# Two routed mixtures: a turn's outputs added to the token sums by an indirect adding DMA in device memory

## What is computed

```python
def moe_swiglu(xn, router, w_gu, w_down):
    top_v, top_i = lax.top_k((xn @ router).astype(jnp.float32), TOP_K)
    w = jax.nn.softmax(top_v, axis=-1)
    comb = jnp.sum(jax.nn.one_hot(top_i, N_EXPERTS, dtype=jnp.float32) * w[..., None], axis=-2)
    out = jnp.zeros_like(xn)
    for e in range(N_EXPERTS):
        out = out + comb[..., e:e + 1] * swiglu(xn, w_gu[e], w_down[e])
    return out
```

## Time and profile before

| | |
|---|---|
| median of 3 runs | 2461.88 us (2461.0 to 2463.66) |
| the profiled execution | 2463.73 us, its span 2461.9 us |
| busy, of the span | PE 92%, PEld 77%, DVE 69%, ACT 54%, POOL 2% |
| mean granted TensorE clock | 0.954 |
| moved by DMA | 605.51 MB, mean 246 GB/s |
| first mixture, turns | about 764 to 1750 us |
| second mixture, turns | about 2145 to 2437 us |

### The profile page before, as it was taken

One profiled execution on the slowest core, in us unless ns is written; L12 is line 12 of the kernel. 1 busy time (PEld: TensorE's weight loads), 2 busy tenths in 40 slices (PEclk: granted clock), 3 DMA queues, 4 the chain that ended last, 5 costly groups with the idle time before them and its releaser, 6 DMA issues.

```text
span 2461.9 us, 29816 instructions
## 1 busy us (share of the span) xinstructions
PE 2261.1 (92%) x11321; PEld 1885.2 (77%) x11321; DVE 1694.6 (69%) x1551; ACT 1335.1 (54%) x1167; POOL 54.8 (2%) x64
## 2 busy tenths in 40 slices
PE   6989999897888999999999999999699789599996
PEld 6748999775676888888888888888589668588884
DVE  4325545576346888888888888888746514588986
ACT  4024333515335777777777777777554213377774
POOL 2000000000000000000000000000000000000000
PEclk9999999999888999999999999999889899599998
DMA  8243455531335999999999999999533242399993
GB/s 273 103 145 132 134 197 173 186 120 52 111 145 194 372 352 375 354 372 352 373 348 375 354 372 354 372 354 364 195 127 112 86 154 84 131 349 355 358 351 129
DMA packets 271625, 605.51 MB, mean 246 GB/s; under 512 B 9232, under 2 KB 34016, under 8 KB 271552
## 3 DMA queue, kind: packets, MB, share of 16 engines
q1 hardware_dynamic: 264944, 582.01, 65.9%
q0 software_dynamic: 6608, 22.49, 2.6%
HBM read 601.31 MB, written 3.15 MB: 246 GB/s over the span
## 4 chain that ended last, share of the span: by engine, by line
PE 79%; DVE 5%; ACT 4%; issue 2%; ACTq 0%; POOL 0%; DVEq 0%
PE ps L678 21%; PE ps L680 21%; PE ps L679 21%; PE ps L621 3%; PE ps L616 2%; DVE w_low L1978 1%; PE ps L940 1%; PE ps L842 1%; ACT w_high L1436 1%; PE ps L869 1%; PE ps L665 1%; PE ps L925 1%; PE ps L697 1%; ACT L1436 1%; PE ps L717 1%
## 5 line engine op out<-in xcount | busy, mean ns | idle before, releaser
L1978 DVE TENSOR_TENSOR w_low<-ring,w_high 128x2048 fp32r<-128x2048 f32 x432 | 983.7, 2289 | 142.2 <-ACT w_high L1436 141.4
L1436 ACT ACTIVATE w_high<-ring 128x2048 fp32r<-128x2048 f32 x432 | 824.0, 1916 | 178.3 <-PE ps L680 178.2
L679 PE MATMUL ps<-w_high,parts 128*128 128x512 f32 (+2 forms) x2024 | 788.9, 390 | 0.0
L678 PE MATMUL ps<-w_high,parts 128*128 128x512 f32 x1816 | 722.5, 398 | 29.7 <-DVE w_low L1978 15.1
L680 PE MATMUL ps<-w_low,parts 128*128 128x512 f32 x1816 | 711.1, 392 | 0.0
L679 PEld LDWEIGHTS ps<-w_high,parts 128*128 128x128 f32 x2024 | 382.7, 189 | 74.1
L678 PEld LDWEIGHTS ps<-w_high,parts 128*128 128x128 f32 x1816 | 342.7, 189 | 109.2 <-issue 24.4
L680 PEld LDWEIGHTS ps<-w_low,parts 128*128 128x128 f32 x1816 | 342.3, 189 | 73.3
L1589 DVE TENSOR_TENSOR w_low<-ring,w_high 128x2048 fp32r<-128x2048 f32 (+2 forms) x93 | 207.3, 2244 | 136.9 <-ACT w_high L1232 136.4
L678 PE MATMUL ps<-XT_high,w_high 128*128 128x256 f32 x896 | 259.0, 289 | 10.1 <-DVE parts L1578 6.2
L1232 ACT ACTIVATE w_high<-ring 128x2048 fp32r<-128x2048 f32 (+2 forms) x93 | 173.2, 1873 | 162.5 <-PE ps L680 123.2
(11 more groups left out here) (368 smaller groups left out, 1887.5 us busy)
## 6 DMA issues: line engine op xcount, KB each, us to landing
ring<-in_od_moe_gu SPq DMA_DIRECT2D x224, 1024.0 KB, 6.9
ring<-in_od_moe_down SPq DMA_DIRECT2D x112, 1024.0 KB, 6.7
ring<-in_w SPq DMA_DIRECT2D x96, 1024.0 KB, 7.2
ring<-in_ev_ffn_gu SPq DMA_DIRECT2D x22, 1024.0 KB, 7.5
ring<-in_xa_wkv SPq DMA_DIRECT2D x8, 2048.0 KB, 7.9
ring<-in_od_pw_w SPq DMA_DIRECT2D x6, 2048.0 KB, 8.7
ring<-in_w_in SPq DMA_DIRECT2D x6, 2048.0 KB, 8.0
ring<-in_ev_ffn_down SPq DMA_DIRECT2D x11, 1024.0 KB, 5.1
```

The source lines that it names most:

```text
L678: mm(out_, xh, wh, start=start, stop=False)
L679: mm(out_, xl, wh, start=False, stop=False)
L1436: A(w_high[:, j % SPLITS, :], ring[:, j % NS, :], ACT.Copy).then_inc(moe_sem(k, "high"), 1)
L1978: V.tensor_tensor(w_low[:, j % SPLITS, :], ring[:, j % NS, :], w_high[:, j % SPLITS, :].bitcast(F32), SUB)\
```

## The change

Inside the loops, the sums are no longer kept in on-chip memory. Ahead of each loop POOL stores `dst` in device memory (`sums`, with 128 spare rows behind the 256 token rows). At half 3 ACT copies the outputs of the turn before to `expert_out`, now in one float32 piece, and POOL issues an indirect DMA that adds these 128 rows to the rows of `sums` that `add_at` names; places of a turn without a token get a spare row. `find_rows` has one more column (`FILLED`), from which `places` on DVE computes the next turn's places (`next_at`), and `move_places` moves them to `add_at` at half 15, after the adding DMA of this turn has landed. In turn 0 all rows go to spare rows. The scatter matmuls, `outputs_low`, the four adds and the transposes of picks leave the loops. Behind a loop POOL reads the sums back to `dst`, and the last turn's outputs are added as before: `pick_last` makes its one-hot matrix once more, PE transposes it, scatters, and DVE adds after a wait for the sums.

```diff
-SCATTER_AT = (6, 8, 10, 11)
 TURN_PICKS_AT = 12
+FILLED = 5
+UNFILLED = 1024.0
...
-        gates = sb("gates", [P, 120])
+        gates = sb("gates", [P, 128])
...
+        rows_at, add_at, next_at = (sb(n, [P, 1], I32) for n in ("rows_at", "add_at", "next_at"))
+        expert_in, expert_out = w_(4096, D), w_(5120, D)
+        sums = {k: nc.dram_tensor(f"sums{k}", (T + P, D), F32, kind="Internal").ap() for k in (1, 2)}
...
-            def expert_rows(k, source, ready, value):
+            def expert_rows(k, source, ready, value, dst):
                 pool.wait_ge(S(ready), value)
                 pool.dma_start(row_store[k].rearrange("(a p) d -> p a d", p=P), source[:, :, :]).then_inc(S("rows_stored"), 16)
-                pool.wait_ge(S("rows_stored"), 16 * k)
+                if k == 2:
+                    pool.wait_ge(S("xs_ready"), 10)
+                pool.dma_start(sums[k][0:T, :].rearrange("(a p) d -> p a d", p=P), dst[:, :, :]).then_inc(S("rows_stored"), 16)
+                pool.dma_start(sums[k][T:T + P, :], dst[:, 0, :]).then_inc(moe_sem(k, "rows_added"), 16)
+                pool.wait_ge(S("rows_stored"), 32 * k)
+                pool.wait_ge(moe_sem(k, "rows_added"), 16)
                 pool.wait_ge(moe_sem(k, "turns_ready"), 1)
                 turns = pool.value_load(count[0:1, k - 1:k], min_val=MOES[k]["groups"], max_val=2 * MOES[k]["groups"])
                 with pool.Fori(0, turns) as it:
 
+                    pool.wait_ge(moe_sem(k, "outputs_by_act"), it + 1)
+                    pool.sem_inc(S("rows_asked"), 1)
+                    pool.indirect_dma_start(sums[k], bass.IndirectOffsetOnAxis(add_at[:, 0:1], 0), expert_out[:, :], None,
+                                            compute_op=ALU.add).then_inc(moe_sem(k, "rows_added"), 16)
                     pool.wait_ge(moe_sem(k, "rows_wanted"), it + 1)
...
+                pool.wait_ge(moe_sem(k, "rows_added"), turns * 16 + 16)
+                pool.sem_inc(S("rows_asked"), 1)
+                pool.dma_start(dst[:, :, :], sums[k][0:T, :].rearrange("(a p) d -> p a d", p=P)).then_inc(S("rows_back"), 16)
...
                             if half == 0:
                                 if ch == C - 1:
-                                    pe.wait_ge(moe_sem(k, "added"), it * 4 + 4)
                                     turn_rows(it + 1)
+                                if ch == 0:
+                                    pe.wait_ge(moe_sem(k, "outputs_by_act"), it + 1)
                                 pe.wait_ge(moe_sem(k, "hidden_split"), it * C + (ch + 1))
...
-                        if j in SCATTER_AT:
-                            scatter(it, SCATTER_AT.index(j))
-                        if j == TURN_PICKS_AT:
-                            turn_picks()
                         if j == ROWS_AT:
                             find_rows(it + 1)
 
+                turn_picks()
                 for i in range(4):
-                    scatter(turns, i)
-                pe.wait_ge(moe_sem(k, "added"), turns * 4 + 4)
+                    scatter(i)
+                pe.wait_ge(S("added"), 4 * k)
...
-                def outputs_high(turn):
+                def outputs(turn):
 
                     act.wait_ge(moe_sem(k, "read"), turn * N + SPLITS)
-                    A(y_high.rearrange("p (a n) -> p a n", a=2), ps[:, 2:4, :], ACT.Copy).then_inc(moe_sem(k, "outputs_by_act"), 1)
+                    act.wait_ge(moe_sem(k, "rows_added"), turn * 16 + 16)
+                    A(expert_out.rearrange("p (a n) -> p a n", a=2), ps[:, 2:4, :], ACT.Copy).then_inc(moe_sem(k, "outputs_by_act"), 1)
...
+                def places():
+
+                    V.tensor_scalar(next_at[:, :], ps[:, 7, FILLED:FILLED + 1], UNFILLED, SPARE, ADD, ALU.min)
+
+                def move_places(turn):
+
+                    dve.wait_ge(moe_sem(k, "rows_added"), turn * 16 + 32)
+                    V.tensor_copy(add_at[:, :], next_at[:, :]).then_inc(moe_sem(k, "places_moved"), 1)
+
                 def rows_wanted(turn):
                     dve.wait_ge(moe_sem(k, "rows_found"), turn)
+                    dve.wait_ge(moe_sem(k, "places_moved"), turn)
+                    places()
...
-                V.memset(picksT[:, :, :].bitcast(F32), 0.0).then_inc(moe_sem(k, "picks_ready"), 1)
                 pick(0)
                 gathered_low(0)
+                places()
...
                     for j in range(N):
-                        if j == EMPTY_AT:
-                            outputs_low(it)
-                        if j - 3 in SCATTER_AT:
-                            add(it, SCATTER_AT.index(j - 3))
                         if j == TURN_PICKS_AT + 3:
-                            picks_ready(it)
                             pick(it + 1)
+                            move_places(it)
...
-                outputs_low(turns)
+                pick_last(turns - 1)
+                picks_ready()
+                outputs_low()
+                dve.wait_ge(S("rows_back"), 16 * k)
                 for i in range(4):
-                    add(turns, i)
-                dve.wait_ge(moe_sem(k, "added"), turns * 4 + 4)
+                    add(i)
+                dve.wait_ge(S("added"), 4 * k)
...
+            step(V.tensor_scalar(CBS[:, :, FILLED:FILLED + 1], CBS[:, :, TOKEN:TOKEN + 1], -UNFILLED, None, ADD))
+            step(V.tensor_scalar(SPARE, CBS[:, 0, TOKEN:TOKEN + 1], float(T), None, ADD))
+            V.tensor_copy(add_at[:, :], SPARE)
```

More of the change, by code:

```diff
@@ L293, in program @@
         RK = gates[:, 72:106].rearrange("p (a e) -> p a e", e=17)
[L294 to L297, removed]
+        CBS = gates[:, 106:118].rearrange("p (a e) -> p a e", e=6)
+        GS = gates[:, 118:122]
+        SPARE = gates[:, 122:123]
+        rows_at, add_at, next_at = (sb(n, [P, 1], I32) for n in ("rows_at", "add_at", "next_at"))
+        expert_in, expert_out = w_(4096, D), w_(5120, D)
+        sums = {k: nc.dram_tensor(f"sums{k}", (T + P, D), F32, kind="Internal").ap() for k in (1, 2)}
         row_store = {k: nc.dram_tensor(f"row_store{k}", (T, D), F32, kind="Internal").ap() for k in (1, 2)}
@@ L590, in _ @@
                 row(0, ins["ln_b_2"][0, j].partition_broadcast(P))
-            expert_rows(2, H, "h_ready", 3)
+            expert_rows(2, H, "h_ready", 3, XS)
             pool.wait_ge(S("h_final"), 1)
@@ L889, in gather @@
                     for tc in range(2):
-                        mm(ps[:, 7, 0:M], PR[:, tc, :], CBS[:, tc, 0:M], start=(tc == 0), stop=(tc == 1))
+                        mm(ps[:, 7, 0:FILLED + 1], PR[:, tc, :], CBS[:, tc, :], start=(tc == 0), stop=(tc == 1))
                     for kc in range(KC):
@@ L900, in find_rows @@
                     for tc in range(2):
-                        last = mm(ps[:, 7, 0:TOKEN + 1], PR[:, tc, :], CBS[:, tc, :], start=(tc == 0), stop=(tc == 1))
+                        last = mm(ps[:, 7, 0:FILLED + 1], PR[:, tc, :], CBS[:, tc, :], start=(tc == 0), stop=(tc == 1))
                     last.then_inc(moe_sem(k, "rows_found"), 1)
@@ L911, in turn_picks, with scatter @@
                 def turn_picks():
+                    pe.wait_ge(S("last_picked"), k)
                     for tc in range(2):
                         last = nc.tensor.transpose(ps[:, 7, T + tc * P:T + (tc + 1) * P], PR[:, tc, :], IDENT)
-                    last.then_inc(moe_sem(k, "picks_turned"), 1)
-                def scatter(turn, i):
+                    last.then_inc(S("picks_turned"), 1)
+                def scatter(i):
                     if i == 0:
-                        pe.wait_ge(moe_sem(k, "outputs_by_vector"), turn + 1)
-                        pe.wait_ge(moe_sem(k, "picks_ready"), turn + 1)
+                        pe.wait_ge(S("outputs_by_vector"), k)
+                        pe.wait_ge(S("picks_ready"), k)
                     if i >= 2:
-                        pe.wait_ge(moe_sem(k, "added"), turn * 4 + (i - 1))
+                        pe.wait_ge(S("added"), 4 * (k - 1) + (i - 1))
                     columns = slice(i % 2 * 512, i % 2 * 512 + 512)
@@ L1403, in gathered_high, with last_outputs_high @@
                     last.then_inc(moe_sem(k, "gathered_high"), 1)
-                def outputs_high(turn):
+                def outputs(turn):
                     act.wait_ge(moe_sem(k, "read"), turn * N + SPLITS)
-                    A(y_high.rearrange("p (a n) -> p a n", a=2), ps[:, 2:4, :], ACT.Copy).then_inc(moe_sem(k, "outputs_by_act"), 1)
+                    act.wait_ge(moe_sem(k, "rows_added"), turn * 16 + 16)
+                    A(expert_out.rearrange("p (a n) -> p a n", a=2), ps[:, 2:4, :], ACT.Copy).then_inc(moe_sem(k, "outputs_by_act"), 1)
+                def last_outputs_high():
+                    act.wait_ge(moe_sem(k, "read"), turns * N + SPLITS)
+                    A(y_high.rearrange("p (a n) -> p a n", a=2), ps[:, 2:4, :], ACT.Copy).then_inc(S("last_outputs"), 1)
                 gathered_high(0)
@@ L1426, in experts @@
                         if j == EMPTY_AT:
```

(28 more changed lines are left out.)

6 lines of the change are left out of this document (3 added, 3 removed).

## The result

The changed kernel takes 2439.77 us in the median of its first four runs (2435.98 to 2443.8), the kernel before 2462.77 (2461.0 to 2463.98): a ratio of 0.9907, with a 95% interval of 0.989 to 0.9925. That is 23.0 us less. The profiled execution took 2435.98 us with a span of 2434.2.

What follows compares the result with a forecast made beforehand. PE's instruction stream was taken to bound each turn. Off PE -24.5 us, ends and starts +0.3, gave -24.2 from the 2461.88 us median: 2438 us (ratio 0.990), own range 2433 to 2444, 8-in-10 range 2430 to 2459.

Steps and rivals of the forecast that it cites:

- What bounds it: In the turns of both mixtures: PE's instruction stream sets the length, PE busy 121.93 of 123.00 us and 71.93 of 73.00.
- Off PE, 2.04 us a turn: Per turn, eight scatter matmuls (1.81 us) and two transposes of picks (0.23) leave PE; 24.5 us over 12 turns.
- To DMA, 2.7 us of the engines: Per turn, one adding DMA of 128 rows, taken as twice the gather's 1.35 us of all 16 engines.
- free time of 8.0 us: First mixture's turn: 44.61 MB at 395 GB/s take 112.9 of 120.9 us, leaving 8.0 us of DMA time.
- cover of 9.4 us: First mixture: a weight lies ready 9.4 us before it is wanted, so a DMA jam of 2.7 us is hidden.
- prices for a slow add: Engine time over 8.0 us a turn is lost: gain gone at 10 us, 2533 us in all at 16.
- The new waits: Five: ACT at half 3, DVE at half 15, POOL's gather, PE's first down half, DVE behind each loop; all expected hidden.
- Ends and starts, +0.3 us: Behind the loops, in the routing and at first loads: small operations and copies, -0.4 to +1.0 us, taken as +0.3.
- Rival 1: In the turns: splits close behind PE, or the start of a turn, give back half the gain; 2450 us, chance 0.10.
- Rival 2: Weight loads: DMA is at its ceiling at 363 GB/s; +11 to +27 us, 2473 to 2489, chance 0.08.
- Rival 3: The adding DMA is slow in itself, by engine time or by landing late at half 15; 2490 or 2533 us, chance 0.11.
- Rival 4: Start of a turn: DVE is lighter and PE's wait (up to 0.9 us) goes; 11 us more gain, 2427, chance 0.03.

Runs made afterwards that it cites:

- the reference: The changed kernel run once more, unchanged, as the reference of the follow-up runs on its chip: 2440.25 us, ratio to the kernel before 0.9896.

## Why the prediction was right

The forecast was 2438 us, a ratio of 0.990; it is 2439.8 and 0.9907. The sum was 24.2 us; the mixtures gave 22.9. The 23.0 of the medians agree with that more closely than they need to: each of the stretches outside the mixtures moved by 6 us and more from profile to profile, which no term covers.

*What bounds it.* Right, and shown from both sides: eight matmuls back on PE bring back 1.9 us a turn, 4.2 us of work back on DVE bring 0.3.

*Off PE, 2.04 us a turn.* Measured 1.92 and 1.97, on the mean 1.93, so the term was 0.1 us a turn too high, 1.3 us in all. Its two sizes hold. Eight steps of 0.2267 are 1.81. The transposes are 0.22: in the turn of the earlier trace rows the next product follows the first transpose by 0.14 us, and the step behind it is 0.08 longer than 0.2267.

```profile
1050.53 0.38 PE L914 MATMUL ps<-const,work 128*128 128x128 f32 x2
1050.67 0.47 PE L678 MATMUL ps<-w_high,parts 128*128 128x512 f32 x1
1050.98 0.39 PE L679 MATMUL ps<-w_high,parts 128*128 128x512 f32 x1
```

What fell short is the sentence "I count the full 2.04", which has the splits follow a shorter stream without a wait. Once a turn they do not. PE's weight load waits 0.24 us for DVE's split, and the next step is 0.32 us instead of 0.23 (changed kernel, timeline of one turn):

```profile
1028.19 0.19 PEld L694 LDWEIGHTS ps<-w_high,parts 128*128 128x128 f32 x1 [0.24 <-DVE w_low L2012]
1028.20 0.48 PE L694 MATMUL ps<-w_high,parts 128*128 128x512 f32 x1
...
1028.52 0.39 PE L695 MATMUL ps<-w_high,parts 128*128 128x512 f32 x1
```

The lists of waits of the kernel before and of the one with the scatters back have no such entry. It gives back 0.1 us of the 2.04.

*To DMA, 2.7 us of the engines.* Measured 2.65. The doubling was a guess from logic, with no row behind it; that it held so closely is luck. The free time of 8.0 us in the first mixture, and the 5.6 of the second that the experiments worked out by the same rate, foretold the growth with four adds (2.5 and 5.0 against 2.0 and 5.3), and the cover of 9.4 us, of which a load now uses 0.8 more, held the rest. (The prediction's own prices for a slow add take 8.0 us for the second mixture too, and so were too low there.)

*The new waits.* None of the five shows in the changed kernel's list of waits. The add was issued at 1009.05 and landed 10.9 us later, near 1020; DVE's copy of places stands at 1045.06 and waits for nothing. There were 25 us of room.

*Ends and starts, +0.3 us.* The net is +0.3, but by luck. The first mixture won 0.8 us beyond its eight turns, 0.6 of it behind the last gather, which nothing here explains. The second lost 1.1 at its start. In both kernels PE waits 6.80 us there and the first products behind the wait start 0.43 us apart; before, six steps were slow, in the changed kernel fourteen are, 8 x 0.20 = 1.6 us. The first 10 us ran at a granted clock of 0.67 instead of 0.85. The prediction had no term for either.

*The rivals.* Rival 1 (half of the gain lost) did not occur, but its mechanism, splits that run close behind PE, is the one that gave back the 0.1 us a turn. Rival 2 is refuted for this kernel: a whole turn with two adding DMAs runs at 376 GB/s with PE unhurt, and with four ACT waits for loads, at 380. The ceiling decides somewhere between two and four times the DMA time that the change needs. The 358 GB/s a core of the Trainium skill (DMA: Bandwidth & Descriptors, Where 436 GB/s comes from) does not bind here; the kernel before was above it already, with 363 over a whole turn. Rival 3 would have needed an add of 10 us to lose the gain; it is 2.65. Rival 4 did not occur, though what it priced is there: the wait at the start of a turn is worth 1.1 us a turn, but a lighter DVE does not remove it (the entry in the list of waits is the same before and after); it takes two edits.

## What to carry to other kernels

Where one engine's stream has no gaps, a change is worth what it takes off that stream, start to start, less what the engines behind it then fail to keep up with (0.1 us of 2.04 here); what a neighbour gets rid of was worth 0.3 us of its 4.2, and nothing while the stream had its old length. A DMA share of 1.00 did not mean that DMA was full: the rate of a burst with many loads queued, set against the bytes of a turn, told the free time to about 1 us. Judge an edit by the length of the stage it touches and not by the run's total alone; one edit here came with a median 9 us lower and did not change its own turns, and another lengthened them by 0.3 us under a total that did not move.

## What the runs showed of the hardware

The stretches outside the mixtures hold no code of the change, yet they are what spreads the profiled runs. The rows of the first mixture are stored at 723.3 to 729.5 us in the twelve profiles, and the stretch between the mixtures varies more than that. From the first load behind the first mixture to the load of the second memory on POOL's timeline it took 174.4 us before, 171.4 in the changed kernel, and 165.9 with PE's work put back. The tables of stretches from 30 to 60 us behind that load, of the changed kernel and of that one:

```profile
1775.00:1805.00 30.00, 28.77 (x123) 22.26 (x122) 14.52 (x23) 13.12 (x26) 0.00 (x0) 0.77 0.26 81
```

```profile
1794.00:1824.00 30.00, 28.77 (x172) 24.12 (x171) 16.66 (x27) 17.63 (x30) 0.00 (x0) 1.00 0.40 140
```

PE is busy for the same 28.77 us, but with 123 matmuls at a granted clock of 0.77 and with 172 at 1.00. In the profiles of the twelve runs shown here this part took 166 us or 171 to 177, and nothing between. That is some 6 us or more, a quarter of the whole gain. In the profiles it accounts for the 4 us too few of one experiment, for the 5 us that the total hid in another, and for 5.9 of the 11.5 us of a third. Which of the two a run gets, whether an edit elsewhere sways it, and whether the changed kernel's wider range comes from it, was seen in one profile of each kernel only and stays open.

An adding DMA of 128 rows of 4 KB took 2.65 us of the 16 engines against 1.35 for the gather of the same rows, 2.2 us of issue on POOL against 2.25, and landed after 10.9 us (the median of twelve; 11.0 in the reference) against 8.9. While the four adds of a turn ran, the bytes moved fell from 395 to 274 GB/s, with the engines' busy share at 1.05 in both stretches.
